# Two token halves for the last output tiles before a residual: a transformer kernel on one core

## The reference, cut to what matters

```python
def rmsnorm(x, g):
    y = xf * lax.rsqrt(jnp.mean(xf * xf, axis=-1, keepdims=True) + EPS)
    return (y * g).astype(x.dtype)

def swiglu(x, w_in, w_out):
    gu = x @ w_in
    return (jax.nn.silu(gu[..., :D_FF]) * gu[..., D_FF:]) @ w_out        # D_FF = 2816
...
# first block
h = h + 0.5 * rmsnorm(swiglu(rmsnorm(h, gn[0]), ffn_w_in[i, 0], ffn_w_out[i, 0]), gn[1])
u = rmsnorm(h, gn[2])
y = mlstm_mixer(u, ...)                                    # ends in y @ w_out
h = h + rmsnorm(y, gn[3])                                  # transition 1 begins in here
h = h + 0.5 * rmsnorm(swiglu(rmsnorm(h, gn[4]), ffn_w_in[i, 1], ffn_w_out[i, 1]), gn[5])   # transition 2
# second block
h = h + 0.5 * swiglu_2(rms_norm(h, ffn1_norm[l]), ffn1_w_gate[l], ffn1_w_up[l], ffn1_w_down[l])
...                                                        # attention + retention, feed-forward, norm
```

## Time and profile before

| what | value |
|---|---|
| median of three runs | 2073.49 us (2068.9 to 2075.01) |
| profiled execution, whole time | 2071.98 us |
| its span in the trace | 2069.9 us |
| its mean granted TensorE clock | 0.981 of full |
| busy share TensorE / VectorE / ScalarE / GpSimd | 96 / 58 / 46 / 44% |
| chain that ended last: TensorE / VectorE / ScalarE / GpSimd | 81 / 8 / 3 / 2% |

### The profile page before, as it was taken

One profiled execution on the slowest core, in us unless ns is written; L12 is line 12 of the kernel. 1 busy time (PEld: TensorE's weight loads), 2 busy tenths in 40 slices (PEclk: granted clock), 3 DMA queues, 4 the chain that ended last, 5 costly groups with the idle time before them and its releaser, 6 DMA issues.

```text
span 2069.9 us, 35347 instructions
## 1 busy us (share of the span) xinstructions
PE 1977.5 (96%) x12886; PEld 1750.6 (85%) x12886; DVE 1194.8 (58%) x1640; ACT 948.9 (46%) x1603; POOL 919.2 (44%) x514
## 2 busy tenths in 40 slices
PE   7899999899998899999989999999999999999998
PEld 7899999887776699987868999787776678999787
DVE  5766650185254877781077778315846537777601
ACT  4466642233423466662255666323436434666422
POOL 3244454444314455564444555544442033555541
PEclk9999999899999999999999999999999999999999
DMA  5233332213212133333322333333321022333331
GB/s 151 59 101 101 102 108 87 82 44 92 72 42 82 51 94 109 101 104 102 100 61 72 102 111 115 92 97 101 83 53 42 11 82 62 102 111 101 103 101 51
DMA packets 342477, 177.84 MB, mean 86 GB/s; under 512 B 18652, under 2 KB 338007, under 8 KB 342383
## 3 DMA queue, kind: packets, MB, share of 16 engines
q1 hardware_dynamic: 340528, 175.46, 29.4%
q10 hardware_dynamic: 1854, 1.07, 0.2%
HBM read 174.42 MB, written 2.10 MB: 85 GB/s over the span
## 4 chain that ended last, share of the span: by engine, by line
PE 81%; DVE 8%; issue 5%; ACT 3%; POOL 2%; DMA 0%; SPq 0%; ACTq 0%; POOLq 0%; DVEq 0%
PE ps L2089 41%; PE ps L2235 33%; POOL wlo L434 2%; DVE wa L1514 1%; DVE E L1539 1%; DVE xop_f L1289 1%; PE ps L2117 1%; DVE xlo L1236 1%; PE ps L2714 1%; PE ps L2696 1%; PE ps L2673 1%; DMA raw<-in_ffn_w_in 0%; PE ps L2677 0%; ACT PR L931 0%; ACT xop L594 0%
## 5 line engine op out<-in xcount | busy, mean ns | idle before, releaser
L434 POOL TENSOR_TENSOR wlo<-raw,whi 128x1024 fp32r<-128x1024 f32 x192 | 486.1, 2541 | 647.3 <-ACT whi L546 646.8
L2235 PE MATMUL ps<-xop,whi 128*128 128x256 f32 (+1 forms) x4032 | 723.3, 282 | 11.6 <-DVE wlo L1355 5.9
L2235 PEld LDWEIGHTS ps<-xop,whi 128*128 128x128 f32 x4032 | 621.2, 190 | 13.5 <-DVE wlo L1355 6.4
L2235 PE MATMUL ps<-xop,wlo 128*128 128x256 f32 (+1 forms) x2016 | 567.3, 281 | 0.0
L480 POOL TENSOR_TENSOR wlo<-raw,whi 128x512 fp32r<-128x512 f32 x212 | 285.3, 1350 | 222.2 <-ACT whi L619 222.1
L2235 PEld LDWEIGHTS ps<-xop,wlo 128*128 128x128 f32 x2016 | 382.1, 190 | 0.0
L2089 PE MATMUL ps<-xop,whi 128*128 128x512 f32 (+1 forms) x1120 | 325.9, 351 | 14.0 <-POOL wlo L434 8.8
L546 ACT ACTIVATE whi<-raw 128x1024 fp32r<-128x1024 f32 x176 | 183.5, 1052 | 263.7 <-PE ps L2089 255.1
L2089 PE MATMUL ps<-xhi,whi 128*128 128x512 f32 (+2 forms) x720 | 248.1, 376 | 36.9 <-DVE xlo L1236 19.2
L2089 PE MATMUL ps<-xop,wlo 128*128 128x512 f32 (+1 forms) x880 | 280.3, 351 | 0.0
L2089 PE MATMUL ps<-xlo,whi 128*128 128x512 f32 (+2 forms) x720 | 239.2, 364 | 0.0
(11 more groups left out here) (355 smaller groups left out, 2659.8 us busy)
## 6 DMA issues: line engine op xcount, KB each, us to landing
raw<-in_ffn_w_in SPq DMA_DIRECT2D x88, 512.0 KB, 3.7
raw<-in_ffn_w_gate SPq DMA_DIRECT2D x44, 512.0 KB, 3.7
raw<-in_ffn_w_up SPq DMA_DIRECT2D x44, 512.0 KB, 3.7
raw<-in_ffn_w_out SPq DMA_DIRECT2D x32, 512.0 KB, 3.8
raw<-in_ffn_w_down SPq DMA_DIRECT2D x32, 512.0 KB, 4.1
raw<-in_a_w_in SPq DMA_DIRECT2D x24, 512.0 KB, 3.7
raw<-in_w_in SPq DMA_DIRECT2D x19, 512.0 KB, 3.8
raw<-in_ffn_w_out SPq DMA_DIRECT2D x16, 384.0 KB, 3.3
```

Of the source, the lines that this page charges most:

```text
L434: pool.tensor_tensor(wlo[:, u % SLOTS, :], raw[:, u % SLOTS, :], whi[:, u % SLOTS, :].bitcast(F32), ALU.subtract).then_inc(lo_done, 1)
L2235: ins = pe.matmul(ps[:, bank_, 0:h], w[l][:, k * P:(k + 1) * P], x[r][:, k * h:(k + 1) * h], start=start and k == 0 and q == 0, stop=k == ...
```

## The change

In both transitions the last output tiles are computed in two halves of 256 tokens, HW = 256: three tiles in transition 1 (`SPLIT[1] = 3`), one in transition 2. First the first halves of these tiles, then the second halves, with the same weights, still in their slots. The norm of the output (sums, root, reciprocal, spread) is made for each half: the first half's within the products of the second halves. `dve_transition`, `act_transition`, `pool_transition` then scale, add, and make `xhi` and `xlo` for all eight tiles of the first half, and after that of the second half, all 256 wide. VectorE reads the spread reciprocal from PSUM (banks 6 and 5), not from `rbc`. `first_halves` takes the place of `first_tiles`: three units instead of two are multiplied as operands arrive, the third three k-tiles behind, over the first half and then the second. The norm of the coming feed-forward adds squares in pairs (`pair_squares`, three additions) and takes 20 one-column sums in the fourth unit, before its second and third k-tile, with the spread before the seventh. In the queues of ScalarE and GpSimd the splits of units u_next+1 to u_next+3 (u_next is the next feed-forward's first unit) stand between steps of the halves.

```diff
+SPLIT = {1: 3, 2: 1}
+LAG = 3
+HW = SEQ // 2
...
+    def out_steps(i):
+        s = SPLIT.get(i, 0)
+        return [(j, None) for j in range(KD - s)] + [(j, half) for half in range(2) for j in range(KD - s, KD)][:2 * s]
...
+    def pool_transition(pool, i, u, u_next):
+        pool_lo(pool, u, u_next + 2)
+        pool_res_half(pool, i, 0, 1, 4)
+        pool_lo(pool, u_next + 2, u_next + 3)
+        pool_res_half(pool, i, 0, 4, KD)
+        pool_lo(pool, u_next + 3, u_next + 4)
+        pool_res_half(pool, i, 1, 1, KD)
...
-        pool_lo(pool, u0 + AHEAD, u0 + 2 * NCONV)
+        pool_lo(pool, u0 + (SLOTS if i in (1, 2) else AHEAD), u0 + 2 * NCONV)
...
+    def act_transition(act, i, u0, per, rms, norm, name, g0):
...
+        def x_hi(k, half):
+            act.wait_ge(res_s["h_ready"], res + KD * half + k + 1)
+            act.activation(half_tile(xhi, k, half), half_tile(hT, k, half), ACT.Copy, scale=gain(name, g0 + k)) \
+               .then_inc(s["hi_ready"], 1)
+        last = KD + SPLIT[i] - 1
+        act_root_half(act, rms, 0)
+        for q in range(2):
+            if q < SPLIT[i] - 1:
+                act_out_step(act, i, SEQ, False, u0, per, None, KD + q)
+            split_to(act, u_next + 1 + q - AHEAD)
+        x_hi(0, 0)
+        x_hi(1, 0)
+        act_out_step(act, i, SEQ, False, u0, per, None, last)
+        x_hi(2, 0)
+        x_hi(3, 0)
+        act_root_half(act, rms, 1)
+        x_hi(4, 0)
+        split_to(act, u_next + 3 - AHEAD)
+        for k in range(5, KD):
+            x_hi(k, 0)
+        for k in range(KD):
+            x_hi(k, 1)
+            act.activation(tile(sqbuf, k, SEQ), tile(hT, k, SEQ), ACT.Square).then_inc(s["sq_ready"], 1)
...
+    def dve_out_step(v, i, n, value, u0, per, gains, add, norm, p):
+        s, at = out_s, out_at[i]
+        j, half = out_steps(i)[p]
+        if p != KD:
+            last_half = out_steps(i)[p - 1][1] if p > 0 else None
...
+            a = part(acc, 0, n, last_half)
+            v.tensor_tensor(a, a, part(sq, (j + 1) % 2, n, last_half), ALU.add).then_inc(s["acc_done"], 1)
...
+    def dve_transition(v, i, value, u0, per, gains, rms, norm, name, g0):
...
+        def scaled(k, half):
+            if k == 0:
+                v.wait_ge(r_s["spread"], r_at[rms]["spread"] + half + 1)
+            if k >= 2:
+                v.wait_ge(s["h_ready"], at["h_ready"] + KD * half + k - 1)
+            v.tensor_tensor(half_tile(wa, k % 2, half), half_tile(value, k, half), ps[:, SPREAD_BANK[half], 0:HW], ALU.mult) \
+             .then_inc(s["t_ready"], 1)
...
+        first = KD + SPLIT[i] - 1
+        dve_recips(v, rms, 0)
+        for half in range(2):
+            scaled(0, half)
+            v.wait_ge(s["t_ready"], at["t_ready"] + KD * half + 1)
+            h = half_tile(hT, 0, half)
+            v.tensor_tensor(h, h, half_tile(wa, 0, half), ALU.add).then_inc(s["h_ready"], 1)
+            for k in range(1, KD + 2):
+                if k < KD:
+                    scaled(k, half)
+                if half == 0 and SPLIT[i] == 3 and k in (2, 4):
+                    step(KD + k // 2 - 1)
+                if half == 0 and k == 5:
+                    step(first)
+                if half == 0 and k == 6:
+                    dve_recips(v, rms, 1)
+                if k >= 2:
+                    lo(k - 2, half)
+        pair_squares(v, norm, 3)
...
-        free_ffn(v)
-        dve_res(v, 1, SEQ, m1["y"], R1, 2, "norm_gains", 32)
-        for k in range(1, KD):
-            sum_square(v, 2, k, SEQ)
...
+    def first_halves(pe, i, rms, norm, banks, units):
+        at = norm_at[norm]["x_ready"]
+        def multiply(b, u, k, half):
+            pe.wait_ge(norm_s["x_ready"], at + KD * half + k + 1)
...
+        for k in range(KD + LAG):
+            for b, u, lag in zip(banks, units, (0, 0, LAG)):
+                if k == lag:
+                    pe.wait_ge(lo_done, u + 1)
+                if lag <= k < KD + lag:
+                    multiply(b, u, k - lag, 0)
+            if k == 1:
+                sum_half(pe, i, 1)
+            if k == 3:
+                spread_half(pe, rms, 1)
+        for k in range(KD):
+            for b, u in zip(banks, units):
+                ins = multiply(b, u, k, 1)
...
+            for k in range(KD):
...
+                if p == KD and k == 2:
+                    sum_half(pe, 1, 0)
+                if p == KD and k == KD - 2:
+                    spread_half(pe, R1, 0)
...
-        sum_out(pe, 1, SEQ)
-        spread(pe, R1)
-        pe.wait_ge(r_s["ready"], r_at[R1]["ready"] + 1)
         pe_ffn(pe, 1, 2, N2)
```

More of the change, by code:

```diff
@@ L728, in out_done, with act_out_step @@
         return 6 if per == 3 and j < 2 else per * (j + 1)
-    def act_out(act, i, n, add, u0, per, norm=None):
+    def act_out_step(act, i, n, add, u0, per, norm, p):
         s, at = out_s, out_at[i]
[L734 to L740, removed]
+        j, half = out_steps(i)[p]
+        act.wait_ge(s["acc_done"], at["acc_done"] + p + (1 if p > KD else 2))
+        if add:
+            act.wait_ge(s["v_ready"], at["v_ready"] + p + 3)
+            value = tile(hT, j, n)
+        else:
+            if half == 0:
+                act.wait_ge(s["half_done"], at["half_done"] + j - KD + SPLIT[i] + 1)
@@ L741, in act_out @@
             else:
                 act.wait_ge(unit_done, STARTED + u0 + out_done(j, per))
[L743 to L746, removed]
+            value = out_bank(i, p, n, half)
+        act.activation(part(sq, j % 2, n, half), value, ACT.Square).then_inc(s["sq_ready"], 1)
@@ new lines, in act_out_step, with act_out @@
+        if norm is not None:
+            act.activation(tile(xhi, j, n), value, ACT.Copy, scale=gain(norm[1], j)).then_inc(norm_s["hi_ready"], 1)
+    def act_out(act, i, n, add, u0, per, norm=None):
+        split_to(act, u0 - 1)
+        for p in range(KD):
+            j, half = out_steps(i)[p]
+            if half is None:
+                split_to(act, u0 + max(per * (j + 1) - 1, 5 if per == 3 else 0))
+            else:
+                split_to(act, u0 + per * (KD - SPLIT[i]))
+            act_out_step(act, i, n, add, u0, per, norm, p)
@@ L2124, in sum_out, with sum_half @@
         column_sums(pe, [(acc, 0), (sq, (KD - 1) % 2 * TOK)], n)
+    def sum_half(pe, i, half):
+        steps, c0 = KD + half * SPLIT[i], 2 * half
+        last = (KD - 1) % 2 * TOK
+        pe.wait_ge(out_s["acc_done"], out_at[i]["acc_done"] + KD + 2 + half * (SPLIT[i] - 1))
+        pe.wait_ge(out_s["sq_ready"], out_at[i]["sq_ready"] + steps)
+        for q, (buf, o) in enumerate(((acc, 0), (sq, last))):
+            for c in (c0, c0 + 1):
+                ins = pe.matmul(ps[:, 7, c + 1:c + 2], buf[:, o + META + c * P:o + META + (c + 1) * P], ones[:, 0:1],
+                                start=q == 0 and c == c0, stop=q == 1, skip_group_check=True)
+        ins.then_inc(r_s["sums"], 1)
@@ new lines, in sum_squares @@
+    def sum_squares(pe, i, part):
+        if part == 0:
+            pe.wait_ge(norm_s["summed"], norm_at[i]["summed"] + 1)
+        else:
+            pe.wait_ge(norm_s["sq_ready"], norm_at[i]["sq_ready"] + KD)
+        for k in ((0, 2, 4), (6, 7))[part]:
+            for c in range(CH):
+                ins = pe.matmul(ps[:, 7, c + 1:c + 2], sqbuf[:, k * TOK + META + c * P:k * TOK + META + (c + 1) * P],
+                                ones[:, 0:1], start=k == 0 and c == 0, stop=k == KD - 1, skip_group_check=True)
+        if part == 1:
+            ins.then_inc(r_s["sums"], 1)
@@ L2215, in pe_ffn @@
                         ins.then_inc(unit_done, 1)
[L2216 removed]
+        whole = NU_DOWN - (len(FFN_PIECES) if i == 1 else 0)
+        for j in range(6, whole):
             m, q = DOWN_UNITS[j]
@@ L2222, in pe_ffn @@
             ins.then_inc(unit_done, 1)
+        if i == 1:
+            for half in range(2):
+                half_of_tile(half)
     def pe_fast(pe, i):
```

187 lines of the change are left out of this document (132 added, 55 removed).

## The result

The changed kernel takes **2077.72 us** (median of 20 runs, 2073.00 to 2087.23); the kernel before, on the same chips, 2073.22 (20 runs, 2067.93 to 2076.84). The ratio is 1.0033 with a 95% interval of 1.0022 to 1.0044: slower, by about 0.3%, where 5.1 us off was forecast. (The ratios here are formed from the single runs; they are not the quotient of the two medians.) The profiled execution of the changed kernel took 2085.19 (span 2083.4). The 20 run times lie in two groups, near 2076.5 and near 2085.3, and this profile is of the upper one; experiment 10 has one of an execution of 2074.67.

What follows compares the result with a forecast made beforehand. TensorE was taken as busiest, with the second spread's time deciding each transition. Gains of 1.9 us (transition 1) and 3.2 (transition 2) made 5.1 off, 2066.9 profiled, predicted median 2068.4 us, range 2060 to 2077.

Steps and rivals of the forecast that it cites:

- Up to the second spread: Fourth unit of each transition, first product through second spread: products, 12 and 8 sums, spread; 7.1 us, replacing 10.8.
- the late end of the three units: First three feed-forward units, both halves, after the last output product: forecast to end at 23.2 us (transition 1), 22.0 (transition 2).
- The second spread decides: Both transitions: the time of the coming norm's reciprocal spread sets the Strassen start; TensorE work pulled ahead gains nothing.
- nothing changes behind rbc: From the second spread's rbc to the Strassen stage: same length as before, TensorE only waits longer for the same wb.
- The products start within 1 us of the last output product: Start of both transitions: products resume at 0, where they used to start 8.6 us after the old end.
- the wait for `acc`: First half, transition 1: TensorE idles some 3.6 us behind k = 1 until the acc addition lets the second half's sums run.
- The lock between VectorE and GpSimd: VectorE operations with both inputs in SBUF wait for a running GpSimd one to end, and alternate; xlo held beside subtractions.
- the half prices: 256-wide operations: GpSimd addition 0.74 plus about 0.2 us, VectorE 0.34 (0.415 less overlap), TensorE product 0.118.
- Full overlap: First rival: the lock seldom strikes, TensorE never waits after 0; gain 6.8 us per transition, about 2060; chance 0.20.
- The dear half addition: Third rival: 256-wide GpSimd additions take up to 1.73 us, deciding from 1.05; about 2081 to 2089; chance 0.18.
- nothing left, by the clock: Second rival: low-clock dips twice per transition in the paced second half, 4 x 1.4 us, cancel the gain; 2073; chance 0.18.
- the paced second half: Second-half k steps of the first three units: TensorE sets the pace, 1.06 us a step, 8.5 us in all.

Runs made afterwards that it cites:

- experiment 10: The changed kernel run again unaltered, for a profile from its lower group of run times; 2078.26 us, ratio 1.0026 to the kernel before.
- Kernel 1: Changed kernel, but the coming norm summed as before, by linked additions and one block of 16 sum instructions; 2068.61 us, ratio 0.9972 to the kernel before.
- kernel 2: Changed kernel with its 40 sum instructions in five groups of 8 between k-tiles, spread before the eighth; 2075.60 us, ratio 1.0003 to the kernel before.
- 3: Kernel before, no halves, with pair additions and the 20 sums (40 instructions) in one block; 2086.56 us, ratio 1.0063 to the kernel before.
- 8: Kernel 6 with the second spread before the fourth unit's fifth k-tile instead of the seventh; 2064.19 us, ratio 0.9958 to the kernel before.
- 9: Kernel 6 with the second spread behind the fourth unit's last k-tile instead of before the seventh; 2068.68 us, ratio 0.9979 to the kernel before.
- kernel 4: Changed kernel with the split and subtraction for u_next+3 moved behind the second half's additions; 2078.95 us, ratio 1.0025 to the kernel before.
- 7: Kernel 1 plus the split and subtraction for u_next+3 moved behind the second half's additions; 2068.63 us, ratio 0.9973 to the kernel before.
- 6: Kernel 1 with one output tile instead of three in halves in transition 1; 2068.02 us, ratio 0.9963 to the kernel before.
- kernel 5: Kernel 1 plus the later u_next+3 split and, in transition 1, later second-half sums and spread; 2077.11 us, ratio 1.0015 to the kernel before.

## Why the prediction was wrong

**The step that failed** is "Up to the second spread": "k = 0 (0.7), 12 sums (1.45), k = 1 (0.7), 8 sums (0.97), k = 2 to 5 (2.8), spread (0.45): 7.1". It took 13.85 in both transitions of the first profile, 12.3 and 10.7 in the other. In the second profile the two are 8.8 us more than the forecast's 14.2; the median missed by 9.3.

- *The count.* The earlier trace rows show 1.93 us for x16. I took them for 16 sums; they are 8 (four token chunks, two sources), two instructions each. The price of one instruction, 0.12, was about right (0.107 here), but the 20 sums are 40 of them. It could be seen in the code beside the row. The "eight" of `sum_half` are instructions too, of four matmuls, so their 0.96 came out near (0.78); only the 20 were counted as calls. In kernel 2 the 40 take 3.94 at the full clock where the forecast had 1.45 + 0.97: 1.5 us a transition, 1.8 by the price of 0.107.
- *The clock.* I priced every product there at 0.234. They cost up to 0.44, since the granted clock falls at the block of 24. Kernels 1, 2 and 3 show it: the same halves with 16 instructions keep 1.00, the same 40 in groups of 8 keep 1.00, a block of 40 without halves loses it. Why such a block brings the low clock although the engine is busy, no run shows. It costs 4.9 us a transition in the slower profile, 3.4 and 1.8 in the other.

Kernel 1 has neither, and its 2068.61 is the predicted time almost to the digit; part of that is luck, since its own stretch is 6.4 where 7.1 was forecast, 1.3 over both transitions, which makes up for the late end of the three units below.

**The steps that held.**
- The second spread decides, and nothing changes behind rbc: shown by 8 against 9, and by 36.9 us in both profiles.
- The products start within 1 us of the last output product; the wait for `acc` is 3.2 (3.6 forecast).
- The lock between VectorE and GpSimd (three 512-wide additions take 4.0 beside one subtraction of kernel 4 and 1.89 without one, so one of them waits for most of it; that the two engines alternate was not seen by itself), and the half prices: GpSimd 0.73 free and 0.87 on the mean (0.74 and 0.2 forecast), VectorE's scaled product 0.41 in its record (0.415 less an overlap forecast), additions and products alike.
- The ends of three units: 24.5 and 21.7 (23.2 and 22.0 forecast). Of the 1.3 in transition 1, 1.0 lies in the clock behind the `acc` wait. Eight instructions of sums and the 15 half-wide products behind them took 1.87 and 3.41, where the forecast's prices give 0.96 and 1.77. In the profiles of kernels 2, 7 and 10 the same wait of 3.2 is followed by a shorter low stretch (1.05 and 2.70 to 2.83), and there three units end after 23.4 to 23.5.
- Term by term, transition 1: -1.9 + 6.75 + 1.3, and 0.3 less at its start (the moved sums and transposes cost 1.1, not 1.4), 5.85, against 5.9 measured. Transition 2: -3.2 + 6.75 - 0.3, and 1.5 from a down-projection window at a granted clock of 0.91 that lies ahead of it (1.00 in the kernel before): 4.75, against 4.85.

**The rivals.** Full overlap (2060) is out: xlo waits, three units end at 24.5 and not at 18.3. The dear half addition (2081 to 2089) is out: 0.87, under its break-even of 1.05. The second, "nothing left, by the clock" (2073), named the right resource in the wrong place: it looked for dips behind idle gaps in the paced second half. A dip behind the `acc` wait came; the costly one came behind work that kept TensorE busy. None of the three had the fourth unit, and so the range ended at 2077, 0.7 below the median.

## What to carry to other kernels

Count instructions, not calls: where a row gives a price for a group, work out from the code how many calls the group is, before the price is used for another number of them. A block of one-column matmuls ahead of something that decides was dear twice here, by itself and by the clock behind it. Keeping it short gained the most (linked additions on an idle VectorE cut 40 instructions to 16, at no cost where no subtraction met them); breaking it up with products saved only the clock. And place the one instruction that the next stage waits for as early as its inputs allow: moving the spread by 12 products moved each transition by 2.45 and 2.86 us.

## What the hardware showed that was not expected

- The granted clock fell to 0.50 in or behind a block of 24 or 40 one-column instructions although TensorE was busy 1.00 in every window. The Trainium skill (TensorE: Matmul & The Clock Gate, section "Part 1: The HAM clock gate") names two states of the clock, 1.2 and 2.4 GHz. The trace agrees: a product costs 0.44 at the one and 0.234 at the other, 1.9 times.
- Forty such instructions in groups of 8 between products kept it at 1.00. A block of 16 kept it in both transitions of kernels 1, 6, 8 and 9 and in transition 1 of kernel 7; it lost it in both of kernel 5 and in transition 2 of kernel 7, and in all three of these TensorE had just waited 0.9 for held additions. No run here tells where the border is.
- The Strassen stages, 1416 matmuls each, last 167.0, 168.1, 168.6 or 169.6 us, with different lengths in two executions of the same kernel; a stretch at 0.50 at the start is 1.5 of it.
